# Weights of differential attention by head: each head's attention between the projections of the next

## The chip, the cores and the metric

One NeuronCore of a Trainium2 chip runs the whole program in one launch. The metric is the device time of that launch in microseconds (us), and of the kernel before three runs are given. PE is the matrix engine (TensorE), DVE the vector engine, ACT the scalar engine, POOL the general one; SP is the queue that issues the DMA loads.

## The reference, cut to what matters

The program is a model of four layers: differential attention with a SwiGLU layer, an RWKV-7 mixer with a mixture of experts, and two layers of sparse attention beside a gated recurrence. The change touches only the first, an attention over `T` = 272 positions (16 meta tokens and 256 inputs) of width 1024 with 8 heads:

```python
qkv = jnp.einsum('bld,de->ble', x, w_in)
q, k, v = jnp.split(qkv, 3, axis=-1)
q = q.reshape(B, Lp, H, 2, Dh)          # 8 heads, 2 halves of 64
k = k.reshape(B, Lp, H, 2, Dh)
vf = v.reshape(B, Lp, H, Dv)            # 8 heads of 128
s = jnp.einsum('bqhcd,bkhcd->bhcqk', qblk, k) * scale
s = s - slopes[None, :, None, None, None] * dist
p = jax.nn.softmax(s, axis=-1)
a = p[:, :, 0] - lam * p[:, :, 1]
o = jnp.einsum('bhqk,bkhe->bqhe', a, vf)
o = o * lax.rsqrt(jnp.mean(o * o, -1, keepdims=True) + SUBLN_EPS) * subln_g * (1.0 - lam_init)
return jnp.einsum('ble,ed->bld', o.reshape(B, L, H * Dv), w_o)
```

## The kernel before, in words

Every engine has one list of instructions, written out by a function per layer (`attention_pe`, `attention_act`, `attention_dve`), and runs it in order. An engine waits only for counters (semaphores) that others raise. `bank` gives a product one of the eight PSUM banks, `b=` a fixed one, and a new owner waits until the one before has been read.

A projection is computed from operands that are split in two parts each: `high` lets ACT round a 128x1024 piece of weights to fp32r (`wh`, L301), `low` lets DVE take the rest (`wl`, L310), and `mm3` adds up three fp32r matmuls (L158 to L160). A unit of 128 output columns is 8 chunks of the contraction times 3, thus 24 matmuls of 272 columns. `H`, the input, lies transposed in 8 chunks and is split in the same way into `at_xs`. Weights come as a stream, `SA`: SP loads 1 MB into one of 3 raw slots, which are two pieces, and a raw slot is free again when `low` has run on its last piece. The split pieces have 4 places (`NPART`), and a place is free when the unit that used it is done.

The first layer runs in three stages, one behind the other:

1. The start. SP issues the parameters (`PAR`), constants (`CB`), all of `H`, three loads of weights and `dist` (the distances). ACT and DVE split `H`, then four pieces; PE waits for both.
2. The projections. 16 units make q and k (transposed, `at_q`, `at_k`), the first four of them chunk by chunk together (`project_units`). Then v is made the other way round, positions on the partitions (`at_v`): four groups of 256 columns, 3 blocks of positions (`QT`: 96, 96, 80), 72 matmuls of 256 columns each.
3. The attention loop over 24 items (8 heads times 3 blocks of query positions). Per item PE makes two scores (`scores`, L558), DVE adds the distances and takes the row maximum (`first`, L705 to L711), ACT takes exponentials (`exps`, L634), DVE combines the two softmaxes (`second`, L721 to L727), PE transposes the result (`turned`, L569) and ACT copies it (L646, L647). Once per head PE multiplies with v (`values`, L577), DVE copies the result (`keep`, L731) and ACT squares it (L655). PE runs `scores` three items ahead of `turned`.

Then 8 matmuls add up the squares of all heads (L594), DVE and ACT make the factors (L741 to L745), PE spreads them (L600), DVE scales the heads (L748), and the output projection begins (`attn_o`). `busy_pe` (L420) is a helper that issues plain fp32 matmuls of 512 columns whose result nobody reads; the norm behind the layer uses it.

## Time and profile before

| What | us |
|---|---|
| median of 3 runs (2877.8 to 2885.52) | 2882.27 |
| the profiled execution | 2887.5 |
| its span, from the first to the last instruction | 2885.7 |
| of it: until PE's first matmul | 19.2 |
| projections of q, k and v, until the first scores | 85.4 |
| attention loop and sums of squares, until the factors | 100.8 |

The last three rows are the stretches at 0 to 19.2, 19.2 to 104.6 and 104.6 to 205.4 us. The other 2680 us of the span, from the factors on, are the rest of this layer and the three others. Sums and durations from the trace belong to the profiled execution, which is 5.2 us above the median.

### The profile page before, as it was taken

To read this page: it belongs to the slowest core of one execution; us is meant where nothing else is said; L and a number is where in the kernel's file an instruction comes from. 1 tells how busy PE (TensorE), PEld (TensorE's weight loads), DVE (VectorE), ACT (ScalarE), POOL (GpSimd) and SP (SyncE) were. 2 spreads that over 40 slices of the span, in tenths; PEclk is the share of its full clock that TensorE was granted. 3 is DMA by queue.
4 is the path that set the end of the run, shared out by engine and by line. 5 is a ranking of instruction groups with operands and counts; after the bars stand their busy time and mean duration, and the time that the engine had idled before them with its cause. 6 is when DMAs were issued, how large, how long until landed. Compare 5 with 4: busy or idle time off the path is not lost.

```text
span 2885.7 us, 49498 instructions
## 1 busy us (share of the span) xinstructions
PE 2687.2 (93%) x21078; PEld 2216.2 (77%) x21078; DVE 2045.1 (71%) x2943; ACT 1541.5 (53%) x2245; POOL 101.4 (4%) x124
## 2 busy tenths in 40 slices
PE   7779999999898999999999999998999989999988
PEld 7649997688876766666666666667969988978977
DVE  4565546664435889898898989895856865757864
ACT  3334442622123777777777777774446454446443
POOL 0000000010003100000000000000000101000001
PEclk9759999999988999999999999999999999999999
DMA  6203553300022799898999989893525634524532
GB/s 206 74 0 117 176 171 98 108 21 4 4 102 75 297 348 349 332 364 335 344 352 348 351 330 364 333 346 102 153 58 149 186 113 123 154 80 145 167 118 96
DMA packets 244413, 547.66 MB, mean 190 GB/s; under 512 B 24492, under 2 KB 187784, under 8 KB 200924
## 3 DMA queue, kind: packets, MB, share of 16 engines
q1 hardware_dynamic: 242204, 541.54, 53.3%
q8 instruction: 169, 2.77, 0.4%
q0 software_dynamic: 1984, 2.89, 0.4%
q14 instruction: 56, 0.46, 0.0%
HBM read 540.46 MB, written 1.05 MB: 188 GB/s over the span
## 4 chain that ended last, share of the span: by engine, by line
PE 75%; DVE 15%; ACT 6%; issue 2%; DMA 2%; DVEq 0%; SPq 0%; ACTq 0%
PE PS L158 20%; PE PS L160 20%; PE PS L159 20%; DVE wl L310 3%; ACT wh L301 3%; PE PS L1066 1%; PE PS L349 1%; PE PS L2379 1%; PE PS L1810 1%; PE PS L577 1%; DVE mix L1359 1%; DMA raw<-in_w_in 1%; DVE mix L1357 1%; PE PS L1836 1%; PE PS L1094 1%
## 5 line engine op out<-in xcount | busy, mean ns | idle before, releaser
L310 DVE TENSOR_TENSOR wl<-raw,wh 128x1024 fp32r<-128x1024 f32 (+2 forms) x630 | 746.3, 1189 | 411.5 <-ACT wh L301 392.7
L301 ACT ACTIVATE wh<-raw 128x1024 fp32r<-128x1024 f32 (+2 forms) x630 | 643.9, 1026 | 582.6 <-PE PS L160 534.5
L310 DVE TENSOR_TENSOR wl<-early,wh 128x1024 fp32r<-128x1024 f32 x384 | 466.8, 1225 | 55.6 <-ACT wh L301 35.2
L301 ACT ACTIVATE wh<-early 128x1024 fp32r<-128x1024 f32 x384 | 407.0, 1061 | 127.7 <-PE PS L160 118.7
L158 PE MATMUL PS<-b_hn_h,wh 128*128 128x256 f32 (+2 forms) x1312 | 378.5, 288 | 15.1 <-DVE wl L310 8.9
L160 PE MATMUL PS<-b_hn_h,wl 128*128 128x256 f32 (+2 forms) x1312 | 372.3, 284 | 0.0
L159 PE MATMUL PS<-b_hn_l,wh 128*128 128x256 f32 (+2 forms) x1312 | 371.7, 283 | 0.0
L158 PE MATMUL PS<-wh,xe_h 128*96 128x512 f32 x896 | 357.3, 399 | 1.2 <-DVE xe_l L1962 1.2
L160 PE MATMUL PS<-wh,xe_l 128*96 128x512 f32 x896 | 353.7, 395 | 0.0
L159 PE MATMUL PS<-wl,xe_h 128*96 128x512 f32 x896 | 353.4, 394 | 0.0
L158 PEld LDWEIGHTS PS<-b_hn_h,wh 128*128 128x128 f32 (+2 forms) x1312 | 233.4, 178 | 20.6 <-DVE wl L310 10.5
L159 PEld LDWEIGHTS PS<-b_hn_l,wh 128*128 128x128 f32 (+2 forms) x1312 | 233.2, 178 | 0.7
L160 PEld LDWEIGHTS PS<-b_hn_h,wl 128*128 128x128 f32 (+2 forms) x1312 | 233.1, 178 | 0.3
L160 PEld LDWEIGHTS PS<-wh,xe_l 128*96 128x96 f32 x896 | 144.8, 162 | 63.6
L158 PEld LDWEIGHTS PS<-wh,xe_h 128*96 128x96 f32 x896 | 145.1, 162 | 61.1 <-DVE xe_l L1962 1.5
L159 PEld LDWEIGHTS PS<-wl,xe_h 128*96 128x96 f32 x896 | 145.4, 162 | 59.3
L158 PE MATMUL PS<-wh,mh_h 128*96 128x512 f32 x448 | 177.8, 397 | 0.0
L160 PE MATMUL PS<-wh,mh_l 128*96 128x512 f32 x448 | 177.0, 395 | 0.0
L159 PE MATMUL PS<-wl,mh_h 128*96 128x512 f32 x448 | 175.8, 392 | 0.0
L158 PE MATMUL PS<-ff_x_h,wh 128*128 128x272 f32 x352 | 102.1, 290 | 0.5 <-DVE ff_x_l L486 0.3
L160 PE MATMUL PS<-ff_x_h,wl 128*128 128x272 f32 x352 | 101.8, 289 | 0.0
L349 PE MATMUL PS<-mix,raw 128*128 128x272 f32 x384 | 95.4, 410 | 6.8 <-DVE mix L1359 4.0
(473 smaller groups left out, 5127.8 us busy)
## 6 DMA issues: line engine op xcount, KB each, us to landing
early<-in_moe_in SPq DMA_DIRECT2D x128, 1024.0 KB, 4.8
raw<-in_moe_in SPq DMA_DIRECT2D x96, 1024.0 KB, 4.8
early<-in_moe_out SPq DMA_DIRECT2D x64, 1024.0 KB, 4.8
raw<-in_w_in SPq DMA_DIRECT2D x56, 1024.0 KB
raw<-in_moe_out SPq DMA_DIRECT2D x48, 1024.0 KB, 4.9
raw<-in_w_in SPq DMA_DIRECT2D x32, 704.0 KB
raw<-in_attn_w_in SPq DMA_DIRECT2D x12, 1024.0 KB, 5.5
raw<-in_rw_w_rkv SPq DMA_DIRECT2D x12, 1024.0 KB, 5.0
```

Source lines behind the costliest of these rows:

```text
L158: e.matmul(o, wh, xh, start=start, stop=False)
L159: e.matmul(o, wh, xl, start=False, stop=False)
L160: return e.matmul(o, wl, xh, start=False, stop=stop)
L301: act.e.activation(st.two(n)[0], st.raw(n), ACT.Copy).then_inc(*act.sig("hi", st.name, n, sem=f"hi_{st.name}"))
L310: dve.e.tensor_tensor(lo, st.raw(n), hi.bitcast(F32), SUB).then_inc(*dve.sig("lo", st.name, n, sem=f"lo_{st.name}"))
L349: t = pe.e.matmul(PS[:, b, 0:Tn], cols_view(256)(st.slot(m))[:, k, c:c + 128], X[:, k, :], start=k == 0, stop=k == KC - 1)
L577: t = e.matmul(PS[:, b, 0:T], at_v[0:kn, kt, h * 128:(h + 1) * 128], at_t[h % 2][0:kn, kt, :], start=kt == 0, stop=kt == 2)
L1066: x = e.matmul(PS[p:p + CB_, b, f * CB_:(f + 1) * CB_], lhsT[p:p + CB_, f, :], rhs[p:p + CB_, f, :], start=True, stop=True)
L1094: x = e.matmul(PS[p:p + CB_, b, f * CB_:(f + 1) * CB_], a_[d][p:p + 64, f, t], b_[d][p:p + 64, f, t], start=True, stop=True)
L1357: e.scalar_tensor_tensor(X, rw_e[:, k, 1:T + 1], par("mu", 48 + i * 8 + k), H[:, k, :], MUL, SUB).then_inc(*dve.own())
L1359: e.scalar_tensor_tensor(X, rw_e[:, k, 0:T], par("mu", i * 8 + k), X, MUL, SUB).then_inc(*dve.sig("mixed", i, k))
L1810: t = e.matmul(PS[0:CAP, b, :], P1[:, i, e_, :], Ht[x][:, i, c], start=i + x == 0, stop=i + x == 3)
```

## The change

Weights of q, k and v come in a stream of their own, `SQ`, in 24 loads of 128 columns (512 KB, one piece each) into six half slots, in the order q, k, v of head 0, then of head 1, and so on. v of a head is now projected as q and k are, into `at_u` (head by position); PE transposes it in three blocks (`v_turned`) and ACT copies them to `at_v` (`v_taken`). The old v matmuls are gone: 288 of 256 columns are replaced by 192 of 272 columns and 24 transposes.

`attention_order` is PE's list: 32 steps; step `i` holds the unit `i` of the 24 and the item `n = i - 3`: `scores(n)`, `unit(i)`, for every third step `v_turned`, `values` or `sums`, and `turned(n - 2)`. ACT and DVE have loops of the same steps, with the evacuation of all units on ACT. The banks are fixed: scores 0 and 1, transposes 2, values 3, units 4 and 5, the sums of squares 6, turned v 7. The sums of squares are taken head by head. Behind them stand four matmuls of `busy_pe`.

At the start `H` comes in four parts, with the first two pieces of weights between them; `PAR` and `CB` come behind the third piece. Only two units are made chunk by chunk, and PE waits for the constants only before the first transpose.

```diff
+            a = self.after
+            return a and ("lo", a.name, len(a.pieces) - len(a.slots) + 2 * m + 1)
...
-    SA = Stream("A", RAW, PARTS)
-    projection(SA, "qk", A["attn_w_in"][0], 0, 2 * D)
-    for u in range(4):
-        by_half(SA, ("v", u), A["attn_w_in"][0], 2 * D + u * 256, 256)
+    SQ = Stream("Q", [x[:, c:c + 1024] for x in RAW for c in (0, 1024)], PARTS)
+    UNITS = [(what, h) for h in range(8) for what in ("aq", "ak", "av")]
+    for what, h in UNITS:
+        by_cols(SQ, (what, h), A["attn_w_in"][0], ("aq", "ak", "av").index(what) * D + h * 128, 128)
+    SA = Stream("A", RAW, PARTS, after=SQ)
     projection(SA, "attn_o", A["attn_w_o"][0], 0, D)
...
         if n >= len(st.parts):
             act.wait_ge(act.at("used", st.name, n - len(st.parts)))
+        elif st.after:
+            act.wait_ge(act.at("used", st.after.name, len(st.after.pieces) - len(st.parts) + n))
         act.e.activation(st.two(n)[0], st.raw(n), ACT.Copy).then_inc(*act.sig("hi", st.name, n, sem=f"hi_{st.name}"))
...
+    at_u = [tile(f"at_u{n}", T) for n in range(2)]
     ITEMS = [(h, i) for h in range(8) for i in range(3)]
+
+    def attention_order(unit, v_turned, scores, turned, values, sums):
+
+
+        for i in range(len(UNITS) + 8):
+            n = i - 3
+            if 0 <= n < len(ITEMS):
+                scores(n)
+            if i < len(UNITS):
+                unit(i)
+            if i >= 3 and i % 3 == 0 and i <= len(UNITS):
+                v_turned(i // 3 - 1)
+            if n >= 5 and n % 3 == 2 and n // 3 <= 8:
+                values(n // 3 - 1)
+            if 2 <= n < len(ITEMS) + 2:
+                turned(n - 2)
+            if n >= 7 and n % 3 == 1 and n // 3 <= 9:
+                sums(n // 3 - 2)
 
     def attention_pe(pe):
         e = pe.e
-        pe.wait_ge(pe.at("consts"))
         pe.wait_ge(pe.at("psum_zero"))
-        for _ in project_units(pe, SA, "qk", [("qk", u) for u in range(4)], at_xs, T, ("x_lo", "attn")):
-            pass
-        for u in range(4, 16):
-            project_unit(pe, SA, "qk", u, 128, at_xs, T)
-        for u in range(4):
-            bs = [bank("v", u, i) for i in range(3)]
-            for k0 in (0, 4):
-                n, (wh, wl) = piece(pe, SA)
-                for i, (q0, qn) in enumerate(QT):
-                    if k0 == 0 and bs[i][1]:
-                        pe.wait_ge(pe.at(*bs[i][1]))
-                    for k in range(4):
-                        t = mm3(e, PS[0:qn, bs[i][0], 0:256], at_xs[0][:, k0 + k, q0:q0 + qn],
-                                at_xs[1][:, k0 + k, q0:q0 + qn], wh[:, k, :], wl[:, k, :], k0 + k == 0, k0 + k == KC - 1)
-                    if k0 and i < 2:
-                        t.then_inc(*pe.sig("v_mm", u, i))
-                t.then_inc(*used(pe, SA, n))
-            pe.also("v_mm", u, 2)
+
+        def unit(i):
+            what, h = UNITS[i]
+            if i == 0:
+                for _ in project_units(pe, SQ, "", UNITS[0:2], at_xs, T, ("x_lo", "attn"), (4, 5)):
+                    pass
+            elif i > 1:
+                project_unit(pe, SQ, what, h, 128, at_xs, T, b=4 + i % 2)
+
+        def v_turned(h):
+            b, before = bank("v_rows", h, b=7)
+            if before:
+                pe.wait_ge(pe.at(*before))
+            pe.wait_ge(pe.at("consts"))
+            pe.wait_ge(pe.at("av", h))
+            for kt, (k0, kn) in enumerate(QT):
+                t = e.transpose(PS[0:kn, b, kt * 128:(kt + 1) * 128], at_u[h % 2][:, k0:k0 + kn], ident)
+            t.then_inc(*pe.sig("v_rows_mm", h))
 
...
+            pe.wait_ge(pe.at("aq", h))
+            pe.wait_ge(pe.at("ak", h))
             for c in range(2):
-                b, before = bank("scores", n, c, b=(n % 2) * 2 + c)
-                pe.wait_ge(pe.at(*before))
+                b, before = bank("scores", n, c, b=c)
+                if before:
+                    pe.wait_ge(pe.at(*before))
...
-            b, before = bank("turned", n, b=4 + n % 2)
-            pe.wait_ge(pe.at(*before))
+            b, before = bank("turned", n, b=2)
+            if before:
+                pe.wait_ge(pe.at(*before))
             pe.wait_ge(pe.at("diff", n))
...
-            b, before = bank("attn_v", h, b=6 + h % 2)
-            pe.wait_ge(pe.at(*before))
+            b, before = bank("attn_v", h, b=3)
+            if before:
+                pe.wait_ge(pe.at(*before))
             pe.wait_ge(pe.at("turned", 3 * h + 2))
+            pe.wait_ge(pe.at("v_rows", h))
...
-        pe.wait_ge(pe.at("qk", 14))
-        pe.wait_ge(pe.at("qk", 15))
-        for n in range(len(ITEMS) + 6):
-            if n < len(ITEMS):
-                scores(n)
-            if n >= 6 and n % 3 == 0:
-                values(n // 3 - 2)
-            if 3 <= n < len(ITEMS) + 3:
-                turned(n - 3)
-        b, before = bank("subln")
-        pe.wait_ge(pe.at(*before))
-        for h in range(8):
+        def sums(h):
+            if h == 0:
+                bank("subln", b=6)
             pe.wait_ge(pe.at("at_sq", h))
-            t = e.matmul(PS[0:8, b, 0:T], one_of_8[:, 7 - h:15 - h], at_sq[:, h, :], start=h == 0, stop=h == 7)
-        t.then_inc(*pe.sig("subln_mm"))
+            t = e.matmul(PS[0:8, 6, 0:T], one_of_8[:, 7 - h:15 - h], at_sq[:, h, :], start=h == 0, stop=h == 7)
+            if h == 7:
+                t.then_inc(*pe.sig("subln_mm"))
+
+        attention_order(unit, v_turned, scores, turned, values, sums)
+        busy_pe(pe, 4, "subln", at=7)
...
-        act.wait_ge(act.at("h_in"))
-        split_act(act, "attn", H, at_xs[0])
-        for n in range(NPART):
-            high(act, SA)
+
+        def x_high(k):
+            act.wait_ge(act.at("h_in", k // 2))
+            e.activation(at_xs[0][:, k, :], H[:, k, :], ACT.Copy).then_inc(*act.sig("x_hi", "attn", k))
+
+        for k in range(2):
+            x_high(k)
+        for n in range(2):
+            high(act, SQ)
+        for k in range(2, KC):
+            x_high(k)
+        high(act, SQ)
...
-        for u in range(16):
-            high(act, SA)
-            if u % 2:
-                act.wait_ge(act.at("qk.mm", u))
-                e.activation((at_q if u < 8 else at_k)[:, u % 8, :], ps("qk", u), ACT.Copy).then_inc(*act.sig("qk", u))
-        for u in range(4):
-            high(act, SA)
-            high(act, SA)
-            for i, (q0, qn) in enumerate(QT):
-                act.wait_ge(act.at("v_mm", u, i))
-                e.activation(at_v[0:qn, i, u * 256:(u + 1) * 256], ps("v", u, i, p=qn, n=256), ACT.Copy).then_inc(
-                    *act.sig("v", u, i))
+
+        def evacuated(i):
+            what, h = UNITS[i]
+            act.wait_ge(act.at(what + ".mm", h))
+            if what == "av" and h >= 2:
+                act.wait_ge(act.at("v_rows_mm", h - 2))
+            dst = at_u[h % 2] if what == "av" else (at_q if what == "aq" else at_k)[:, h, :]
+            e.activation(dst, ps(what, h), ACT.Copy).then_inc(*act.sig(what, h))
+
+        def v_taken(h):
+            act.wait_ge(act.at("v_rows_mm", h))
+            src = PS[0:96, bank_of["v_rows", h], 0:384].rearrange("p (a b) -> p a b", a=3)
+            e.activation(at_v[0:96, :, h * 128:(h + 1) * 128], src, ACT.Copy).then_inc(*act.sig("v_rows", h))
...
-        for n in range(len(ITEMS) + 6):
-            if n < len(ITEMS):
-                exps(n)
-            if n >= 7 and n % 3 == 1:
-                h = n // 3 - 2
-                act.wait_ge(act.at("attn_v", h))
-                e.activation(at_sq[:, h, :], at_o[:, h, :], ACT.Square).then_inc(*act.sig("at_sq", h))
+        def sums(h):
+            act.wait_ge(act.at("attn_v", h))
+            e.activation(at_sq[:, h, :], at_o[:, h, :], ACT.Square).then_inc(*act.sig("at_sq", h))
+
+        for i in range(len(UNITS) + 8):
+            n = i - 3
+            if 1 <= i <= len(UNITS):
+                evacuated(i - 1)
+            if i >= 4 and i % 3 == 1 and i <= len(UNITS) + 1:
+                v_taken(i // 3 - 1)
             if 3 <= n < len(ITEMS) + 3:
                 turned(n - 3)
+            if i + 3 < len(UNITS):
+                high(act, SQ)
+            elif i < len(UNITS) + 1:
+                high(act, SA)
+            if 0 <= n < len(ITEMS):
+                exps(n)
+            if n >= 6 and n % 3 == 0 and n // 3 <= 9:
+                sums(n // 3 - 2)
...
+
+        def x_low(k):
+            dve.wait_ge(dve.at("x_hi", "attn", k))
+            e.tensor_tensor(at_xs[1][:, k, :], H[:, k, :], at_xs[0][:, k, :].bitcast(F32), SUB).then_inc(
+                *dve.sig("x_lo", "attn", k))
+
+        for k in range(2):
+            x_low(k)
+        for n in range(2):
+            low(dve, SQ)
+        for k in range(2, KC):
+            x_low(k)
+        low(dve, SQ)
         dve.wait_ge(dve.at("consts"))
-        dve.wait_ge(dve.at("h_in"))
-        split_dve(dve, "attn", H, *at_xs)
-        for n in range(NPART):
-            low(dve, SA)
...
-        for u in range(16):
-            low(dve, SA)
-            if u % 2 == 0:
-                dve.wait_ge(dve.at("qk.mm", u))
-                e.tensor_copy((at_q if u < 8 else at_k)[:, u % 8, :], ps("qk", u)).then_inc(*dve.sig("qk", u))
-        for u in range(4):
-            low(dve, SA)
-            low(dve, SA)
-        dve.wait_ge(dve.at("dist"))
...
+            dve.wait_ge(dve.at("dist"))
             dve.wait_ge(dve.at("scores_mm", n))
...
+        for i in range(len(UNITS) + 8):
+            n = i - 3
+            if 0 <= n < len(ITEMS):
                 first(n)
             if 1 <= n <= len(ITEMS):
                 second(n - 1)
-            if n >= 7 and n % 3 == 1:
+            if i + 3 < len(UNITS):
+                low(dve, SQ)
+            elif i < len(UNITS) + 1:
+                low(dve, SA)
+            if n >= 6 and n % 3 == 0 and n // 3 <= 9:
                 keep(n // 3 - 2)
...
     def sync(sp):
         e = sp.e
+        for c in range(4):
+            e.dma_start(flat(H[:, 2 * c:2 * c + 2, :]), A["hT"][:, 2 * c * T:(2 * c + 2) * T]).then_inc(
+                *sp.sig("h_in", c, by=16, sem=f"h_in{c}"))
+            if c < 2:
+                load(sp, SQ)
+        load(sp, SQ)
         e.dma_start(PAR, A["par"]).then_inc(*sp.sig("consts", by=16))
         e.dma_start(CB, A["c_base"]).then_inc(*sp.sig("consts", by=16))
-        e.dma_start(flat(H), A["hT"]).then_inc(*sp.sig("h_in", by=16))
+        load(sp, SQ)
+        e.dma_start(flat(dist), A["c_dist"]).then_inc(*sp.sig("dist", by=16))
+        while sp.piece["Q"] < len(SQ.loads):
+            load(sp, SQ)
         for m in range(NRAW):
             load(sp, SA)
-        e.dma_start(flat(dist), A["c_dist"]).then_inc(*sp.sig("dist", by=16))
```

How the order moves, in three places. First SP's queue from its start (`raw_53` to `raw_55` are the three raw slots), before:

```order
L2882 DMA PAR<-in_par 128x777
L2883 DMA CB<-in_c_base 128x592
L2884 DMA H<-in_hT 128x2176
L290 DMA raw_53<-in_attn_w_in 128x8x256
L290 DMA raw_54<-in_attn_w_in 128x8x256
L290 DMA raw_55<-in_attn_w_in 128x8x256
L2887 DMA dist<-in_c_dist 128x816
L290 DMA raw_53<-in_attn_w_in 128x8x256
```

and with the change:

```order
L2933 DMA H<-in_hT 128x544
L293 DMA raw_53<-in_attn_w_in 128x8x128
L2933 DMA H<-in_hT 128x544
L293 DMA raw_53<-in_attn_w_in 128x8x128
L2933 DMA H<-in_hT 128x544 x2
L293 DMA raw_54<-in_attn_w_in 128x8x128
L2938 DMA PAR<-in_par 128x777
L2939 DMA CB<-in_c_base 128x592
L293 DMA raw_54<-in_attn_w_in 128x8x128
L2941 DMA dist<-in_c_dist 128x816
L293 DMA raw_55<-in_attn_w_in 128x8x128 x2
```

`H` and the first two pieces now stand ahead of the constants, and a load has half the columns.

Second DVE in the middle of the attention, from one item's scores to the next (`at_s_72` and so on are buffers of the items, `wl_57` to `wl_63` the four places of split weights), before:

```order
L705 SCALAR_TENSOR_TENSOR at_s_72<-dist,PS 96x544 [waits attn_mm_pe]
L709 TENSOR_REDUCE at_x_86<-at_s_72 96x2 [waits attn_dve]
L711 TENSOR_SCALAR at_x_86<-at_x_86 96x2 [waits order_dve]
L721 RECIPROCAL at_x_89<-at_x_89 96x2 [waits attn_dve,attn_act]
L723 TENSOR_SCALAR at_x_89<-at_x_89,lam 96x1 [waits order_dve]
L725 TENSOR_SCALAR at_c_83<-at_e_79,at_x_89 96x272 [waits order_dve]
L727 SCALAR_TENSOR_TENSOR at_c_83<-at_e_79,at_x_89,at_c_83 96x272 [waits order_dve]
L705 SCALAR_TENSOR_TENSOR at_s_73<-dist,PS 80x544 [waits attn_mm_pe]
```

and with the change:

```order
L750 SCALAR_TENSOR_TENSOR at_s_73<-dist,PS 80x544 [waits attn_mm_pe]
L754 TENSOR_REDUCE at_x_87<-at_s_73 80x2 [waits attn_dve]
L756 TENSOR_SCALAR at_x_87<-at_x_87 80x2 [waits order_dve]
L766 RECIPROCAL at_x_86<-at_x_86 96x2 [waits attn_dve,attn_act]
L768 TENSOR_SCALAR at_x_86<-at_x_86,lam 96x1 [waits order_dve]
L770 TENSOR_SCALAR at_c_80<-at_e_76,at_x_86 96x272 [waits order_dve]
L772 SCALAR_TENSOR_TENSOR at_c_80<-at_e_76,at_x_86,at_c_80 96x272 [waits order_dve]
L315 TENSOR_TENSOR wl_63<-raw_55,wh_62 128x1024 [waits hi_Q]
L750 SCALAR_TENSOR_TENSOR at_s_74<-dist,PS 96x544 [waits attn_mm_pe]
```

Each item now has one `low` of weights behind it.

Third PE at the end of a head. Before, from `values`:

```order
L577 MATMUL PS<-at_t_84,at_v 128x272 [waits attn_act]
L577 MATMUL PS<-at_t_84,at_v 128x272 x2
L569 MATMUL PS<-CB,at_c_83 96x96 [waits attn_dve]
L569 MATMUL PS<-CB,at_c_83 96x96
L569 MATMUL PS<-CB,at_c_83 80x96
L558 MATMUL PS<-at_k,at_q 96x272 [waits attn_dve]
L558 MATMUL PS<-at_k,at_q 96x272
L569 MATMUL PS<-CB,at_c_80 96x96 [waits attn_dve]
L569 MATMUL PS<-CB,at_c_80 96x96
```

with the change, from the last matmul of a unit:

```order
L162 MATMUL PS<-at_x_h,wl_57 128x272
L606 MATMUL PS<-at_t_84,at_v 128x272 [waits attn_act]
L606 MATMUL PS<-at_t_84,at_v 128x272 x2
L596 MATMUL PS<-CB,at_c_83 96x96 [waits attn_dve]
L596 MATMUL PS<-CB,at_c_83 96x96
L596 MATMUL PS<-CB,at_c_83 80x96
L584 MATMUL PS<-at_k,at_q 96x272 [waits attn_dve]
L584 MATMUL PS<-at_k,at_q 96x272
L160 MATMUL PS<-at_x_h,wh_58 128x272 [waits lo_Q]
```

Before, `values` stands behind scores alone; now a whole unit stands ahead of it, and another behind the next scores.

## Rows read from the trace of the kernel before

**Rows 1.** Page, part 4: shares of the chain that ended last, by engine

```profile
PE 75%; DVE 15%; ACT 6%; issue 2%; DMA 2%; DVEq 0%; SPq 0%; ACTq 0%
```

**Rows 2.** Busy time by stretch: length, each engine (records), PE clock, DMA share, GB/s

```profile
0.00:19.20 19.20, 0.00 (x0) 0.01 (x1) 11.30 (x14) 7.95 (x13) 0.20 (x4) 1.00 0.93 306
19.20:104.60 85.40, 85.16 (x673) 84.79 (x673) 31.70 (x37) 28.96 (x41) 0.00 (x0) 1.00 0.48 155
104.60:205.40 100.80, 69.79 (x233) 35.59 (x232) 70.44 (x178) 42.33 (x157) 0.00 (x0) 0.54 0.04 11
2292.00:2322.00 30.00, 26.93 (x212) 25.24 (x211) 19.48 (x49) 17.63 (x42) 11.18 (x22) 1.00 0.57 175
```

**Rows 3.** Timeline, 8 to 20 us: start, length, instruction [idle before <- releaser]

```profile
9.49 2.66 ACT L501 ACTIVATE at_x_h<-H 128x272 fp32r<-128x272 f32 x8 [7.48 <-DMA H<-in_hT]
...
15.51 2.00 ACT L301 ACTIVATE wh<-raw 128x1024 fp32r<-128x1024 f32 x2 [1.01 <-DMA raw<-in_attn_w_in]
...
16.60 2.36 DVE L310 TENSOR_TENSOR wl<-raw,wh 128x1024 fp32r<-128x1024 f32 x2 [0.65 <-ACT wh L301]
...
19.22 0.56 PE L158 MATMUL PS<-at_x_h,wh 128*128 128x272 f32 x1 [19.22 <-DVE wl L310]
```

**Rows 4.** DMA issues: count, KB each, median us from issue to landing

```profile
raw<-in_rw_a SPq DMA_DIRECT2D x2, 256.0 KB, 3.6
...
PAR<-in_par SPq DMA_DIRECT2D x1, 388.5 KB, 3.2
```

**Rows 5.** Timeline, PE at 20 to 25.5 us and ACT in the projections

```profile
20.03 0.43 PE L158 MATMUL PS<-at_x_h,wh 128*128 128x272 f32 x1
20.26 0.43 PE L159 MATMUL PS<-at_x_l,wh 128*128 128x272 f32 x1
...
25.45 0.29 PE L158 MATMUL PS<-at_x_h,wh 128*128 128x272 f32 x1
...
40.78 1.06 ACT L301 ACTIVATE wh<-raw 128x1024 fp32r<-128x1024 f32 x1 [1.89 <-PE PS L160]
...
46.80 1.06 ACT L301 ACTIVATE wh<-raw 128x1024 fp32r<-128x1024 f32 x1 [1.89 <-PE PS L160]
```

**Rows 6.** Timeline, PE in the attention loop, around one head's end

```profile
139.94 0.71 PE L569 MATMUL PS<-CB,at_c 96*96 96x96 f32 x3
140.58 1.20 PE L558 MATMUL PS<-at_k,at_q 64*80 64x272 f32 x4
...
146.60 3.09 PE L577 MATMUL PS<-at_t,at_v 96*128 96x272 f32 x6 [3.10 <-ACT at_t L647]
```

**Rows 7.** Timeline, DVE in the attention loop, one item

```profile
143.08 0.43 DVE L731 COPY at_o<-PS 128x272 f32<-128x272 f32 x1
143.43 0.71 DVE L705 SCALAR_TENSOR_TENSOR at_s<-dist,PS 80x544 f32<-80x544 f32 x1
...
146.44 0.71 DVE L705 SCALAR_TENSOR_TENSOR at_s<-dist,PS 96x544 f32<-96x544 f32 x1
```

**Rows 8.** Timeline, DVE and PE from the last item's scores to the output projection

```profile
188.69 0.70 DVE L705 SCALAR_TENSOR_TENSOR at_s<-dist,PS 80x544 f32<-80x544 f32 x1
...
192.71 0.50 DVE L727 SCALAR_TENSOR_TENSOR at_c<-at_e,at_x,at_c 80x272 f32<-80x272 f32 x1
...
205.36 0.43 DVE L741 TENSOR_SCALAR n<-PS 8x272 f32<-8x272 f32 x1 [4.67 <-PE PS L594]
...
194.74 1.88 PE L569 MATMUL PS<-CB,at_c 96*96 96x96 f32 x9
...
200.14 5.18 PE L594 MATMUL PS<-at_sq,CB 128*8 128x272 f32 x16
208.51 6.45 PE L600 MATMUL PS<-r,CB 8*128 8x272 f32 x16 [3.18 <-DVE r L745]
214.88 0.59 PE L158 MATMUL PS<-at_x_h,wh 128*128 128x272 f32 x1
```

**Rows 9.** Timeline, PE, 512-column fp32 matmuls of busy_pe behind the norm

```profile
250.89 1.45 PE L426 MATMUL PS<-CB 128*128 128x512 f32 x3
```

More of the change, by code:

```diff
@@ L55 @@
     "ln": "ln_centred ln_var ln_sq ln_root ln_scaled",
-    "attn": "lam_dots lam_exp subln subln_r subln_o subln_root at_sq attn_v scores row_max diff exps turned",
-    "attn_mm": "v_mm scores_mm turned_mm attn_v_mm subln_mm subln_o_mm",
+    "attn": "lam_dots lam_exp subln subln_r subln_o subln_root at_sq attn_v scores row_max diff exps turned aq ak av v_rows",
+    "attn_mm": "v_rows_mm scores_mm turned_mm attn_v_mm subln_mm subln_o_mm",
     "k_norm": "k_k k_sq k_norm k_norm_root k_norm_r k_spread",
@@ L115, with __init__ @@
 class Stream:
-    def __init__(self, name, slots, parts):
-        self.name, self.slots, self.parts = name, slots, parts
+    def __init__(self, name, slots, parts, after=None):
+        self.name, self.slots, self.parts, self.after = name, slots, parts, after
         self.loads, self.pieces, self.of = [], [], {}
@@ L143, in freed @@
         if before < 0:
-            return None
+            a = self.after
+            return a and ("lo", a.name, len(a.pieces) - len(a.slots) + 2 * m + 1)
         pieces = self.loads[before][1]
@@ L731, in keep @@
             e.tensor_copy(at_o[:, h, :], ps("attn_v", h)).then_inc(*dve.sig("attn_v", h))
-        for n in range(len(ITEMS) + 6):
-            if n < len(ITEMS):
+        for i in range(len(UNITS) + 8):
+            n = i - 3
+            if 0 <= n < len(ITEMS):
                 first(n)
@@ L2881, in sync @@
         e = sp.e
+        for c in range(4):
[4 more added lines that the diff above has]
+        load(sp, SQ)
         e.dma_start(PAR, A["par"]).then_inc(*sp.sig("consts", by=16))
         e.dma_start(CB, A["c_base"]).then_inc(*sp.sig("consts", by=16))
-        e.dma_start(flat(H), A["hT"]).then_inc(*sp.sig("h_in", by=16))
+        load(sp, SQ)
+        e.dma_start(flat(dist), A["c_dist"]).then_inc(*sp.sig("dist", by=16))
+        while sp.piece["Q"] < len(SQ.loads):
+            load(sp, SQ)
         for m in range(NRAW):
             load(sp, SA)
-        e.dma_start(flat(dist), A["c_dist"]).then_inc(*sp.sig("dist", by=16))
         if stages < 3:
-            for m in range(NRAW, 20 if stages == 1 else 20 + 30):
+            for m in range(NRAW, 8 if stages == 1 else 8 + 30):
                 load(sp, SA)
```

## The prediction

> **What bounds the kernel now.** I read the page's chain first. PE holds 75% of what ended last [rows 1], so an edit pays where it takes PE time or PE waits away. Then I cut the first layer into its stretches [rows 2]. Up to 19.2 us PE does nothing. In the next 85.4 us it is busy for 85.2, and DVE and ACT for about a third. In the following 100.8 us, the attention loop, PE is busy for only 69.8, and its granted clock is 0.54 where it was 1.00 before: most of that stretch runs at the lower level, 1.2 GHz, so even the 69.8 are about twice what the same work takes at 2.4 GHz. DVE is busy for 70.4 and ACT for 42.3. What PE waits for is seen once per head: 3.10 us ahead of `values`, for ACT's copy of the last transposes [rows 6], because a chain of PE, DVE, ACT, DVE, PE, ACT has to be walked and PE has nothing else to do. So one stretch has PE full and DVE idle, the next has the chain as its bound and a slow PE. The change lays one over the other.
>
> **The start.** Before, `H` is there for ACT at 9.49, the second pair of weight pieces is begun at 15.51 and PE begins at 19.22, behind four `low` [rows 3]. The change needs only two pieces and `H` in front. How fast is the queue? The whole first stretch moves 306 GB/s on the mean [rows 2]; without some 2.5 us in which nothing moves yet that is about 0.35 MB per us. `PAR`, 0.40 MB, lands 3.2 us after its issue at 0.7 [rows 4]; 1.1 of that is its bytes, so 2.1 is fixed. By this, `H` parts 1 and 2 with two pieces (1.6 MB) land at 0.7 + 2.1 + 4.6 = 7.4. The same reckoning puts the end of the 1.8 MB up to `H` before at 8.0, where ACT had it at 9.49, so I add 1.5: 8.9. Then `high` 1.0 and `low` 1.2, halves of a pair [rows 3]: PE begins at 11.1, 8.1 earlier. The unknown is the packet of 512 bytes (128 columns) in place of 1 KB. Nearest row: `rw_a`, 256 KB in packets of 256 bytes, 1024 of them as in a piece here, lands in 3.6 us [rows 4], where fixed part and bytes give 2.8. So a piece costs between nothing and 0.8 more, and at the very worst as much as 1 MB, 1.4 more. I take nothing, as 512 bytes lie nearer to 1 KB in bytes per packet; the other end puts the start at 13.9.
>
> The Trainium skill, "DMA: Bandwidth & Descriptors", section Specifications, gives 512 bytes as the smallest transfer that runs at line rate. By that rule the start stays at 11.1 us; by the bound from the rows it would be up to 2.8 later.
>
> Once started, PE's matmuls come 0.23 apart until about 25.4, 6.2 us after the first, some 27 of them, and from then on a unit of 24 takes (46.80 - 40.78) / 2 = 3.01, 0.125 each [rows 5]. The same ramp is paid after. Units 0 to 2 are 72 matmuls: 6.2 + 45 x 0.125 = 11.8, so the first scores begin at 22.9.
>
> **The 21 steps with unit and item.** PE's share of each piece at full clock is half of its row in the loop [rows 6]: scores 1.20 / 2 = 0.6, transposes 0.64 / 2 = 0.32 (the next instruction starts 0.64 after them), `values` 3.09 / 2 = 1.55. The transposes of v are new: three blocks of 128 columns where 96 take 0.32, so 0.43; the other end is that they don't gain from the clock, 0.85. A sum of squares is 5.18 / 8 = 0.65 [rows 8], I take 0.45. The steps hold 21 units (63.2), 21 scores (12.6), 19 transposes (6.1), 7 turned v (3.0), 6 `values` (9.3) and 5 sums (2.3): 96.5 us, 4.6 per step.
>
> Does DVE keep up? An item costs it 3.01 from start to start [rows 7], a `low` 1.18 [rows 3], `keep` 0.43 [rows 7], once per three steps: 21 x 4.19 + 5 x 0.43 = 90.2, 4.3 per step. It fits, by 6%. ACT is busy 42.3 in the old loop and gets 1.0 for `high`, 0.4 for an evacuation and a sixth of a microsecond for v per step: about 3.3. Do the chains fit? `turned(n - 2)` stands at the end of step n, some 2.8 steps or 12.9 us after its scores began; scores 0.7, first 1.65, exponentials 1.1 and the place of `second` behind the next `first` need about 8.2. `values` comes after a whole unit, 3.0 us, which covers the 3.10 wait. The wait for `lo` is covered by three steps, that for a load by about six (0.5 MB per 4.6 us is 114 GB/s, a third of the rate). A unit's bank is read one step before it is wanted. If any of these covers went, its wait would stand open on PE. So the steps end at 22.9 + 96.5 = 119.4.
>
> **The tail.** Three items are left without units: the first of them starts on DVE at 120.1, and two items with one `low` and one `keep` put item 23 at 127.7. Before, from there to the factors was 205.36 - 188.69 = 16.7 us [rows 8]. Two parts of it go: the transposes of three items queue behind `values` and end at 196.6, 3.4 us after the last `second` at 193.2; alone they need 0.64 (2.7 less). And DVE waits 4.67 for eight sums; the square and one sum are 1.1 (3.5 less). That gives 127.7 + 10.5 = 138.2, at the lower clock, as before. **Gain so far: 205.4 - 138.2 = 67.2 us.**
>
> **Behind the sums.** Before, PE idles 3.18 for the factors, spreads them in 6.45 and starts the output projection at 214.88, at the lower clock [rows 8]. Now four matmuls of 512 columns fill the wait. Two records are one matmul; they follow 0.43 apart at the full clock [rows 9]: 3.4 in all, hidden. At half clock they are 6.9 and delay the factors by 3.7. In return they can give the spreading at full clock (up to 2.8 less) and the first 21 matmuls of the projection (2.1 less, 0.1 each). Between +3.7 and -4.6 I take 0. The three other layers have the same instructions; the banks rotate from another start, so that a few waits there ask for another bank. I cost that at nothing, up to 2 us either way: such waits ask for work one unit or more back.
>
> **Sum:** 2887.5 - 67.2 = 2820.3 for the profiled execution, which stood 5.2 above the median: **2815 us**.
>
> **Rivals.** (A) *DVE becomes the bound.* It is in order: each step it may have to wait for PE's scores, as it does once per head now, and then `low` stands behind it. If 0.7 us of each step are such a wait, a step is 5.0 and 21 steps 105 (+9); with the 1.8 that the copy of a head's scores waits now, in every third step or more, up to 5.4 (+18). For it: only 6% of room. Against: PE's scores stand first in their step and wait for nothing late. 2824 to 2833; chance 0.15.
>
> (B) *PE stays at the lower clock among small pieces: slower than before.* The loop of now is at 0.54 with its short matmuls. At half clock a unit is 24 x 0.23 = 5.5 and the rest doubles: 21 x 5.5 + 66.6 = 182, 86 more: 2901, 19 slower. It decides from 7.8 us per step (4.6 + 67 / 21); half clock would be 8.7. Against it: in the last layers the same pattern, a head's attention between projections, stands at 2292 to 2322 with PE busy for 26.9 of 30 us and a clock of 1.00 [rows 2]. Chance 0.04. The Trainium skill, "TensorE: Matmul & The Clock Gate", section "A second HAM failure mode: psum-queue depth-cycling", tells of a kernel whose PE idles briefly between groups as PSUM banks come round, so that its clock swings between both levels; that would be this rival. Row 2292 speaks against it.
>
> (C) *The overlap doesn't come about*, as one wait holds every step back until the chain has been walked: the gain is then only the start and the cheaper v (85.4 us less 16 units of 3.01 and 2.8 for the ramp leaves 34 for v; 8 units are 24, and the transposes 3), 8 + 7: 2867. All waits that I followed have a step or more of room. Chance 0.04.
>
> **Chances and range.** The forecast with its bounds (start +2.8; transposes of v +3; behind the sums +3.7 or -4.6; tail at full clock, `values` and scores, -3; other layers 2 either way) has 0.77 and goes from 2805 to 2826. To leave out no more than 2 in 10, the range reaches over (A): 2804 to 2834. A difference of 0.3%, 9 us, is about what can be told from no change. Faster 0.95, within it 0.01, slower 0.04.
>
> **What would show it.** PE's first matmul near 11 us; first scores near 23; scores of successive items 4.6 apart with 4.2 and 5.4 in turn; granted clock 1.00 to about 119; PE busy over 95% there and DVE about 90%; the factors' first instruction near 138; the output projection near 148. (A) shows as PE waiting for `diff` or `lo`, DVE without idle time; (B) as 0.23 between a unit's matmuls. I am wrong if steps take over 5.2 us, or if the gain is lost again behind 140 us.

## The result and the profile after

The changed kernel takes **2841.4 us** (median of four runs, 2837.0 to 2842.7), the kernel before 2880.0 on the same chip (four runs, 2876.2 to 2885.5). The ratio is 0.9861, 95% interval 0.9844 to 0.9878: 38.6 us faster. I had forecast 2815 in a range of 2804 to 2834. The sign is right, the size is not, and the time lies outside the range.

The profiled execution of the change took 2837.0 us, with a span of 2835.2 and a mean granted clock of 0.969. It is the fastest of its kernel's runs, and the one shown of before (2887.5) is slower than all four above, so the two executions are 50.5 us apart where the medians are 38.6 apart. The traces tell where the difference lies, the medians how large it is.

The first layer in stretches: windows of the change, to be held against [rows 2]. Columns as there.

```profile
0.00:10.80 10.80, 0.00 (x0) 0.01 (x1) 6.84 (x6) 5.64 (x10) 0.20 (x4) 1.00 0.89 268
10.80:21.70 10.90, 10.88 (x74) 10.73 (x74) 7.60 (x16) 5.32 (x9) 0.00 (x0) 1.00 1.13 317
21.70:119.80 98.10, 98.10 (x713) 83.05 (x712) 83.22 (x170) 61.91 (x175) 0.00 (x0) 1.00 0.45 130
119.80:141.60 21.80, 13.44 (x50) 6.42 (x48) 11.89 (x29) 9.21 (x30) 0.00 (x0) 0.67 0.16 48
```

The stretch from the first scores to the last step is 98.1 us. PE is busy in all of it at a granted clock of 1.00, where the old loop had 0.54. DVE is busy for 83.2 of it.

The start: timeline of the change, beside [rows 3].

```profile
5.37 1.06 ACT L306 ACTIVATE wh<-raw 128x1024 fp32r<-128x1024 f32 x1 [0.99 <-DMA raw<-in_attn_w_in]
8.25 1.06 ACT L306 ACTIVATE wh<-raw 128x1024 fp32r<-128x1024 f32 x1 [1.82 <-DMA raw<-in_attn_w_in]
9.33 1.23 DVE L315 TENSOR_TENSOR wl<-raw,wh 128x1024 fp32r<-128x1024 f32 x1 [1.65 <-ACT wh L306]
10.82 0.57 PE L160 MATMUL PS<-at_x_h,wh 128*128 128x272 f32 x1 [10.82 <-DVE wl L315]
```

The second piece, in packets of 512 bytes, is there for ACT at 8.25, where the forecast had 8.9. The smaller packets cost nothing that can be seen here.

Three steps of PE in the middle of the stretch, timeline; the units stand in the gaps between the rows shown.

```profile
42.16 0.69 PE L584 MATMUL PS<-at_k,at_q 64*80 64x272 f32 x4
45.88 1.54 PE L606 MATMUL PS<-at_t,at_v 96*128 96x272 f32 x6
47.26 0.41 PE L596 MATMUL PS<-CB,at_c 96*96 96x96 f32 x3
47.60 0.70 PE L584 MATMUL PS<-at_k,at_q 64*96 64x272 f32 x4
51.34 0.49 PE L572 MATMUL PS<-CB,at_u 128*96 128x128 f32 x3
51.66 0.41 PE L596 MATMUL PS<-CB,at_c 96*96 96x96 f32 x3
52.00 0.70 PE L584 MATMUL PS<-at_k,at_q 64*96 64x272 f32 x4
55.74 0.37 PE L596 MATMUL PS<-CB,at_c 80*96 80x80 f32 x3
56.04 0.62 PE L614 MATMUL PS<-at_sq,CB 128*8 128x272 f32 x2
56.60 0.69 PE L584 MATMUL PS<-at_k,at_q 64*80 64x272 f32 x4
```

From scores to scores (L584) it is 5.44, 4.40 and 4.60 us: a step with `values`, one with the transposes of v (L572), one with a sum of squares (L614). `values` takes 1.54, half of the 3.09 of [rows 6]. No row has a wait.

The tail and the sums: PE's timeline of the change, beside [rows 8].

```profile
134.98 0.64 PE L596 MATMUL PS<-CB,at_c 80*96 80x80 f32 x3 [2.08 <-ACT at_t L680]
135.55 1.08 PE L614 MATMUL PS<-at_sq,CB 128*8 128x272 f32 x2
136.55 3.09 PE L606 MATMUL PS<-at_t,at_v 96*128 96x272 f32 x6
140.64 1.07 PE L614 MATMUL PS<-at_sq,CB 128*8 128x272 f32 x2 [1.00 <-ACT at_sq L684]
141.64 4.92 PE L431 MATMUL PS<-CB 128*128 128x512 f32 x8
146.49 3.93 PE L624 MATMUL PS<-r,CB 8*128 8x272 f32 x16
150.35 0.39 PE L160 MATMUL PS<-at_x_h,wh 128*128 128x272 f32 x1
```

The output projection begins at 150.35, 64.5 us ahead of its 214.88 in [rows 8]. That is the forecast of 67 within 3 us. **What is missing from the forecast was lost behind it.** The table follows single instructions of DVE through both traces, and through the first experiment, which is told below. The first three columns are their starts, the last two how much earlier than before.

| instruction, place | before | change | e1 | change earlier | e1 earlier |
|---|---|---|---|---|---|
| `rw`, end of the preparation of the scan | 591.90 | 526.09 | 528.17 | 65.8 | 63.7 |
| `mh_l`, head of the experts' layer | 989.46 | 930.73 | 918.83 | 58.7 | 70.6 |
| `Yl`, its end | 1959.78 | 1900.81 | 1888.96 | 59.0 | 70.8 |
| `wl`, in the last two layers | 2448.72 | 2393.90 | 2376.21 | 54.8 | 72.5 |
| `b_rms_s`, the end | 2875.42 | 2824.87 | 2799.37 | 50.6 | 76.1 |

Two places give time back in the change: between the first row and the second, the recurrent layer with its scan, 7.1 us, and behind the third, the last two layers, 8.4. Through the experts' layer, 970 us, nothing moves. In e1 the same two places gain.

### The profile page after: what moved, and what is told of

Its sections match the earlier page's. It is cut to its first block, busy times and chain, and to the rows that moved or that the text cites. A ratio compares the mean times of both kernels' runs of the same rounds, so it can differ in the third digit from the quotient of the medians.

```text
span 2835.2 us, 49373 instructions
## 1 busy us (share of the span) xinstructions
PE 2660.0 (94%) x21014; PEld 2201.3 (78%) x21014; DVE 2039.8 (72%) x2935; ACT 1543.4 (54%) x2257; POOL 97.0 (3%) x124
## 4 chain that ended last, share of the span: by engine, by line
PE 77%; DVE 13%; ACT 6%; issue 2%; DMA 1%; DVEq 0%; SPq 0%; ACTq 0%
PE PS L160 20%; PE PS L162 19%; PE PS L161 19%; DVE wl L315 4%; ACT wh L306 3%; PE PS L354 2%; PE PS L1116 2%; DMA raw<-in_w_in 1%; PE PS L1144 1%; PE PS L1860 1%; PE PS L2429 1%; PE PS L1886 1%; PE PS L1153 1%; PE PS L2401 1%; DVE b_cx L2811 1%
## 5 line engine op out<-in xcount | busy, mean ns | idle before, releaser
L160 PEld LDWEIGHTS PS<-b_hn_h,wh 128*128 128x128 f32 (+2 forms) x1312 | 233.5, 178 | 21.9 <-DVE wl L315 11.1
L161 PE MATMUL PS<-ff_x_l,wh 128*128 128x272 f32 x352 | 101.3, 288 | 0.0
```

Of the source, the lines that this page charges most:

```text
L160: e.matmul(o, wh, xh, start=start, stop=False)
L161: e.matmul(o, wh, xl, start=False, stop=False)
```

## What changed behind the first layer: a counter

The code there is the same, but what `bank` deals out is not. It deals the eight banks from a running counter, `turn[0] % 8`. Before, the counter stood at 29 ahead of the factors; in the change, with fixed banks for units, turned v and sums, it stands at 0. So every product after that which takes its bank from the counter lies three banks further round, while the ones with a fixed bank (`b=`) stay. Where both kinds meet, a product now gets a bank with another owner, and PE, in order, waits until that owner has been read.

One such place in full: in each of the last two layers PE makes `ma` in banks 4 to 7 (L2456), then `rnn` in the same banks, which DVE reads last of all (`rnn_gate`, L2871), then the units `out_a` (L2502) from the counter. PE's timeline of the change there:

```profile
2318.12 0.28 PE L162 MATMUL PS<-b_hc,wl 128*128 128x256 f32 x1
2321.23 0.36 PE L160 MATMUL PS<-b_o,wh 128*128 128x256 f32 x1 [2.83 <-DVE b_m L2871]
```

PE's 2.83 us of idle time are for the first bank of `out_a`, which is one of those four. Windows of the change around it, 4 us each:

```profile
2316.00:2320.00 4.00, 2.40 (x21) 2.19 (x19) 2.00 (x3) 2.88 (x4) 0.00 (x0) 1.00 0.77 241
2320.00:2324.00 4.00, 2.77 (x15) 2.80 (x16) 2.08 (x5) 2.70 (x2) 0.00 (x0) 0.73 0.59 184
2324.00:2328.00 4.00, 4.00 (x31) 4.00 (x30) 0.93 (x1) 1.06 (x1) 0.00 (x0) 0.84 0.29 99
```

The granted clock was 1.00, falls to 0.73 on the mean of the stretch in which PE comes back, and is 0.84 in the next one: 31 matmuls in 4 us against 37 at full clock. So the wait of 2.8 us costs more than 2.8: 0.27 and 0.16 of 4 us each are another 1.7, by estimate. The windows of e1 at the same place:

```profile
2303.80:2307.80 4.00, 4.00 (x37) 4.00 (x36) 2.01 (x3) 2.87 (x4) 0.00 (x0) 1.00 0.76 248
2307.80:2311.80 4.00, 4.00 (x37) 4.00 (x36) 2.31 (x6) 3.64 (x3) 0.00 (x0) 1.00 0.59 189
```

The Trainium skill, "TensorE: Matmul & The Clock Gate", section "A second HAM failure mode: psum-queue depth-cycling", describes a kernel that goes round the PSUM banks, in which PE idles briefly so often that its clock swings between both levels. I had held it against the interleaved steps, where the clock stayed at 1.00. Here, where I had not looked, the 0.73 behind one wait for a bank agrees with it in kind; this is a single wait of 2.83 us and not a frequent short one.

## Experiments

Two theories stood at the start. **Banks:** the 27 us missing are the counter's. **Others:** they come from where the drops of PE's clock fall, whatever the banks, or they are a consequence of the change in the first layer itself (the idle matmuls, the order of the loads, transfers that arrive at other times). All edits are on the changed kernel unless it says otherwise. Ratios are against the kernel before, run on the same chip, with 95% intervals.

**e1: the counter set back to what it was.** From the output projection on, every wait then asks for the same bank and owner as before.

```diff
         busy_pe(pe, 4, "subln", at=7)
+        turn[0] = 29
         pe.wait_ge(pe.at("subln_r"))
```

> The changed kernel, with the rotation of the PSUM banks set, behind the sums of squares, to where it stood in the kernel before (29 banks taken), so that every later wait for a bank asks for the same owner as before. Theory 1 (the 65 us gained in the first layer are partly lost behind it because the banks rotate from another start and PE waits for other banks in the RWKV scan and the last layers): the instructions behind the first layer run 64 to 66 us earlier than before to the very end, and the total gain is 60 to 67 us (about 2817). Theory 2 (the later loss comes from where the drops of the matrix engine's clock fall, whatever the banks): the gain stays near 40 us (2835 to 2845), with the same loss behind 530 us. Theory 3 (the later layers are tied to loads that do not move with the first layer): also near 40 us.

Measured 2814.0 us (five runs, 2811.5 to 2823.7), ratio 0.9784 (0.9764 to 0.9804). One line that computes nothing is worth 27.4 us by the medians; the two ratios, 0.9861 and 0.9784, are 22 us apart, the two traces 25.5. It is also the time that I had forecast for the change.

**e2: the counter alone, in the kernel before.**

```diff
+        turn[0] = 32
         pe.wait_ge(pe.at("subln_r"))
```

> The kernel before, with only the rotation of the PSUM banks set behind the sums of squares to where the changed kernel has it (a multiple of 8). Theory 1 (banks): slower than before by 20 to 27 us, 2900 to 2907, with the loss in the RWKV scan and the last layers. Theory 2 (clock drops) and theory 3 (loads): no difference beyond 5 us from before.

Measured 2898.8 us (six runs, 2897.1 to 2907.5), ratio 1.0074 (1.0056 to 1.0092). 32 deals bank 0 next, as the change does; there is nothing else of the change in it, and it is about 20 us slower by the medians. In the traces, where before stands with one of its longer executions, e2 loses 3.4 us in the recurrent layer and 9.8 behind 2100 us, the two places that were expected. PE's waits between 2320 and 2400 us, first e2, then before:

```profile
PE PS L158 <- DVE b_m L2822: 4.1, 2, 2.8
```

```profile
PE PS L158 <- DVE b_m L2821: 1.7, 1, 1.7
```

The second wait of e2 stands ahead of `out_a`, as long as in the change; before has none there, its 1.7 stands ahead of a matmul of `rnn`:

```profile
2381.14 0.36 PE L158 MATMUL PS<-b_o,wh 128*128 128x256 f32 x1 [2.83 <-DVE b_m L2822]
```

So the rotation makes it, not the new first layer. e1 and e2 together decide for the banks.

**e3: without the idle matmuls** (the `busy_pe` line removed).

> The changed kernel without its four idle matmuls behind the sums of squares. In its trace they ran from 141.6 to 146.5 us and the factors were spread in 3.9 us at the full clock; before, spreading took 6.5. All theories: without them spreading starts 1.5 to 2 us earlier but takes 6.5 us, and the first 20 matmuls of the output projection are at the lower clock: the output projection starts 1 us later to 1 later, and its first units end 1 to 3 us later. Total within 3 us of the changed kernel, if the later layers do not react.

Measured 2836.2 us (2835.6 to 2838.2), ratio 0.9849 (0.9829 to 0.9868): not to be told from the change. Its trace has what was to be seen, PE idle for the factors and their spreading at half speed:

```profile
145.53 7.62 PE L623 MATMUL PS<-r,CB 8*128 8x272 f32 x16 [3.18 <-DVE r L794]
```

It ends at 153.2 where the change has its first projection at 150.35, and 400 us into the trace it is 3.8 us later than the change. Of that only 0.9 is left at the head of the experts' layer, and the median is 5 us better than the change's. One pair of executions can't price so small a part: e5 below, the same code as the change up to the last two layers, is 10.0 us ahead of it at 720 us and 3.7 at the head of the experts' layer. e10 puts the question again where the scan has the banks of before.

**e4: the loads in the old order** (at the start `PAR`, `CB`, the four parts of `H`, then four pieces of `SQ`).

> The changed kernel with SP's queue at the start in the old order: parameters and constants, then H in its four parts, then four pieces of weights, then the distances. From 0.35 MB per us the two first pieces land after 2.85 MB, 3.5 us later than in the change. All theories: PE's first matmul at 14 to 15 us in place of 10.8, everything behind it equally later, total 3 to 4 us slower than the changed kernel.

Measured 2840.5 us (2837.2 to 2840.9), ratio 0.9861 (0.9841 to 0.9881). In the trace PE begins at 14.06, as expected, and the layers behind the first are 3.7 us later than in the change at 400 us and 3.9 at the end, with less than 1 us in the middle of the scan; yet the median is the same. Medians taken at different times differ by some 3 us for reasons of their own (before's own are 2878.9 to 2882.3); a part of that size is read from the trace's start only.

**e5: the counter of before from the last two layers on.**

```diff
     def second_pe(pe, l):
+        if l == 0:
+            turn[0] = 647
         e = pe.e
```

> The changed kernel, with the rotation of the banks set as in the kernel before only from the first of the two last layers on; the RWKV scan keeps the changed rotation. Theory 1a (the loss has two places that add up: 12 us in the scan, 14 in the last two layers, as the traces of the change and of e1 stand against each other): 2826 us, give or take 3. Theory 1b (the loss in the last layers only follows from the state in which the scan leaves the kernel): no better than the change, 2838 to 2843.

Measured 2825.3 us (2820.0 to 2830.0), ratio 0.9813 (0.9797 to 0.9829): by the medians 16.1 us of the 27.4 are in the last two layers. In the trace e5 gains 13.3 us on the change behind the head of the experts' layer.

**e6: `out_a` in banks that are free**, each unit in bank `u`, the counter left as the change has it.

```diff
-            projected(pe, l, "out_a", u, oT)
+            projected(pe, l, "out_a", u, oT, b=u)
```

> The changed kernel with one stage of the last layers on fixed banks: the eight units of out_a take banks 0 to 7 in order, so that the first four of them do not ask for the banks of the contraction rnn, which DVE reads last. The rotation elsewhere is that of the change (eight banks more or less are a full turn). In the trace of the change PE waits 2.83 us for that read, its clock falls, and out_a ends about 5 us later than in e1, in each of the two layers. Theory 1 (this one wait is most of the loss in the last layers): 9 to 11 us faster than the change, 2830 to 2833. Rival (the loss is spread over many small waits): within 3 us of the change.

Measured 2827.4 us (2824.8 to 2830.2), ratio 0.9813 (0.9798 to 0.9828). One call with a fixed bank is worth 14.0 us by the medians; I had expected 9 to 11. Each of the two ratios carries 4 to 5 us of uncertainty, and the two traces are only 8.0 apart, 3.8 of it at the first `out_a` and 4.3 at the second. So this one set of waits is at least half of what the last two layers lose, and by the medians nearly all. PE's waits for `b_m` in both last layers (2200 us to the end), first in the change, then in e6:

```profile
PE PS L160 <- DVE b_m L2871: 9.4, 4, 3.5
```

```profile
PE PS L160 <- DVE b_m L2871: 2.7, 2, 1.5
```

The two that are gone are those ahead of `out_a`, 2.83 and 3.49 us. Part of this comes back a little later, at the first unit of `out`, in both layers; here the first of them, in the change, then in e6:

```profile
2348.26 0.36 PE L160 MATMUL PS<-b_q_r,wh 128*128 128x256 f32 x1 [2.66 <-DVE wl L315]
```

```profile
2344.41 0.36 PE L160 MATMUL PS<-b_q_r,wh 128*128 128x256 f32 x1 [3.43 <-DVE b_cx L2895]
```

With 0.8 us more there in each layer, 4.8 us of the 8.0 are waiting. The other 3.2 fit the clock: in e6 it is 1.00 between 2316 and 2332 us, where the change loses 1.7 by the estimate above, and at the second `out_a` (2768 to 2776 us) the change has 0.62 and 0.95, again 1.7. Where the rest of the 14.0 is, no trace shows.

**e9: the other half, the counter of before for the scan and the experts alone** (`turn[0] = 29` as in e1, and the change's own value, 618, at the head of `second_pe`).

> The complement of e5: the changed kernel with the banks as in the kernel before from the sums of squares to the end of the mixture of experts, so in the scan, and the changed rotation again in the two last layers. If the two places add up (theory 1a), e5's gain of 16 us over the change and this one's make up e1's 27: 2828 to 2832. If the scan's loss is not its own (theory 1b): 2838 to 2843.

Measured 2827.6 us (2825.3 to 2832.3), ratio 0.9822 (0.9803 to 0.9841): 13.8 us. With e5's 16.1 that is 29.9 against e1's 27.4, so the two places are separate and together are the whole. The traces agree more closely: e9 is 12.1 us ahead of the change at the head of the experts' layer and 11.8 at the end, which with e5's 13.3 makes 25 against e1's 25.5. As the experts' layer moved by nothing in the table, this part belongs to the recurrent layer. Not all of it is the scan: e9 is 7.7 us ahead of the change at 720 us, 5.7 at 800 and 12.1 at 860, and e1 likewise (7.4, 5.7, 12.0), so that a part comes behind the scan, where I followed no wait. PE's longest waits in the scan, 590 to 740 us in the change:

```profile
PE PS L1098 <- ACT rw_ru L1353: 10.7, 1, 10.7
...
PE PS L1144 <- DVE sc_lb L1508: 2.7, 1, 2.7
PE PS L1177 <- DVE sc_lb L1508: 2.7, 1, 2.7
```

and in e1, 570 to 725 us:

```profile
PE PS L1099 <- ACT sc_pad L1327: 9.6, 1, 9.6
...
PE PS L1145 <- DVE sc_lb L1509: 0.9, 1, 0.9
PE PS L1191 <- DVE sc_lb L1509: 0.9, 1, 0.9
```

Two waits for DVE's `sc_lb` are 2.7 where they were 0.9. They ask for the fixed banks 4 to 7, which the transposes of the scan (`forward`) take and DVE reads. One stands ahead of the same line in both kernels (L1144, in e1 L1145); the other ahead of `upd` (L1177) in the change and ahead of `y` (L1191), which PE issues later, in e1. They give 3.6 us and the first row 1.1. What follows the first of them in the change is the clock:

```profile
598.76 1.53 PE L1177 MATMUL PS<-rw_ru,sc_n 56*56 56x64 f32 x24 [2.71 <-DVE sc_lb L1508]
```

```profile
594.00:598.00 4.00, 1.89 (x14) 1.70 (x14) 1.84 (x3) 0.10 (x1) 0.00 (x0) 1.00 0.00 0
598.00:602.00 4.00, 3.24 (x61) 3.25 (x63) 3.45 (x16) 0.60 (x1) 0.00 (x0) 0.51 0.02 4
602.00:606.00 4.00, 4.00 (x94) 4.00 (x92) 0.00 (x0) 0.60 (x1) 0.00 (x0) 0.63 0.00 0
```

Windows of 40 us, the change first, then about the same work in before:

```profile
594.80:634.80 40.00, 34.87 (x1002) 34.31 (x1003) 17.19 (x42) 12.48 (x24) 0.00 (x0) 0.88 0.01 3
```

```profile
660.00:700.00 40.00, 36.22 (x1175) 35.45 (x1171) 17.16 (x42) 14.84 (x28) 0.00 (x0) 1.00 0.02 4
```

PE is busy for about as long and gets 1002 matmuls done instead of 1175. The traces of e3, e4, e5 and e6, which have the change's counter in the scan, show the same wait of 2.7 us and behind it a 4 us window at 0.57 to 0.66; those of before, e1, e7 and e9 have the 0.9, and the clock stays at 1.00 there. Behind the second wait the clock falls in the change, e3 and e4 but not in e5 and e6: the same wait does not cost the same in every execution. No run gave the scan's products fixed banks one by one, so what each wait is worth in time stays open.

**e7: e1 and e6 together.**

> e1 (the banks as before from the sums of squares on) with out_a on banks 0 to 7. In e1 only the first unit of out_a was free of the wait; now four are. Theory 1: between e1 and 3 us better, 2811 to 2815. A version that could be kept.

Measured 2816.0 us (2808.2 to 2818.7), ratio 0.9762 (0.9747 to 0.9777). It can't be told from e1: with the counter of before, the first `out_a` units already find free banks, and e1's waits for `b_m` (3.1 us) are hardly more than e6's.

**e8: e7 with another start, 27.**

> As e7, but the rotation two banks further back (27 in place of 29), which no kernel here has had. out_a no longer depends on it. Theory 1 says only that the scan reacts to the rotation: between e7 and 12 us slower, 2812 to 2826. If it is as fast as e7, the scan's loss belongs to the one rotation of the change; if faster, the rotation of the kernel before was not the best.

Measured 2819.8 us (2819.0 to 2823.1), ratio 0.9791 (0.9776 to 0.9806), 4 us behind e7 by the medians, 8 by the ratios, whose intervals just touch. With `out_a` fixed, this start costs little, but it doesn't beat the old one.

**e10: e7 without the idle matmuls.**

> e7 without the four idle matmuls behind the sums of squares, to price this term where nothing behind it reacts. e3's trace had the rest of the program 3.8 us later than the change's, but its median was 5 us better than the change's in another call. If the matmuls pay (they keep the clock up for the spreading and the output projection): 1 to 4 us slower than e7, 2817 to 2820. If not: 2811 to 2815.

Measured 2823.1 us (2820.4 to 2826.7), ratio 0.9799 (0.9781 to 0.9817), against e7's 0.9762: in this pair they are worth 7 us by the medians and 11 by the ratios, where I had expected 1 to 4. In the traces e10 is 3.2 us later at 400 us, of which the spreading explains 2.3 (it ends at 152.6 instead of 150.3). The lag is about 0 at 560 us, 3.2 again at 1963, and 6.9 at 2800. So what is shown of them is 3 to 4 us where they stand (e3 and e10). What they are worth in the whole stays open: 7 us here, nothing in the change against e3.

## Why the prediction was wrong, and where it was right

The order follows the prediction.

- **Start.** PE at 10.8 (forecast 11.1), first scores at 21.7 (22.9). Right, and the end of the range with slow small packets is excluded.
- **Steps.** (119.82 - 21.68) / 21 = 4.67 us (forecast 4.6), the last at 119.8 (119.4). PE never idle, clock 1.00. The pieces at half of their row in the old loop came out at 0.69 for scores (0.60) and 1.54 for `values` (1.55).
- **DVE** was forecast at 90.2 of the 96.5 us and took 83.2 of 98.1. Rival A (DVE as the bound) asked for PE waiting on `diff` or `lo`; PE waited for nothing there, and DVE idled 8.6 us for PE's scores:

```profile
DVE at_s L750 <- PE PS L584: 8.6, 11, 1.3
```

- **Rival B** (a slow PE among small pieces) asked for a step of 7.8 and a low clock: 4.67 and 1.00. **Rival C** (no overlap) asked for 2867 us, 52 more than the forecast, with PE held by a wait in every step. Both are out.
- **Tail.** The factors begin 3.5 us later than forecast, at 141.75, not 138.2: item 23 was on DVE at 129.23, not 127.7, and from there it took 12.5, not 10.5, as DVE's timeline shows:

```profile
129.23 0.72 DVE L750 SCALAR_TENSOR_TENSOR at_s<-dist,PS 80x544 f32<-80x544 f32 x1 [1.05 <-PE PS L584]
...
133.26 0.50 DVE L772 SCALAR_TENSOR_TENSOR at_c<-at_e,at_x,at_c 80x272 f32<-80x272 f32 x1
...
141.75 0.43 DVE L791 TENSOR_SCALAR n<-PS 8x272 f32<-8x272 f32 x1 [1.63 <-PE PS L614]
```

  The term of 10.5 was too small by 2, in two places that the rows of the tail above show. The transposes do take only 0.64, but they begin 1.2 us behind the last `second` (133.26 and 0.50 long), because all transposes now share bank 2 and ACT had first to copy the ones before ([2.08 <-ACT at_t L680]). Behind them a sum of squares (1.08) stands ahead of the last `values`.
- **Behind the sums.** I took 0 between +3.7 and -4.6. The idle matmuls took 4.9 us, mostly beside DVE's work, and the spreading 3.93 in place of 6.45 [rows 8]. The output projection then stood 64.5 us ahead, against a sum of 67.2.
- **"The three other layers have the same instructions; the banks rotate from another start, so that a few waits there ask for another bank. I cost that at nothing, up to 2 us either way."** This is the step that failed. It was 27.4 us by the medians (e1; 22 by the ratios), and about 20 alone (e2). I named the mechanism and gave as its price that "such waits ask for work one unit or more back". That holds between products of the counter, eight of them apart. It does not hold where they meet products in fixed banks, whose reader may be among the latest instructions of DVE, as `rnn_gate` is: 2.83 and 3.49 us of wait ahead of `out_a`, and a lower clock behind. The order of the instructions with their waits was there to be compared over the whole program, and the row that would have priced it was in the trace: how late DVE reads `rnn`.

With the counter set back, e1 was 64.9 us faster than before (2878.9 to 2814.0; 56 to 68 by the ratio's interval), against the 67.2 of the sum. That its 2814.0 meets the 2815 to a microsecond is luck, as before's own median was 3 us lower there; that the rest of the sum holds within its uncertainty is not. In the traces e1 goes on gaining behind the first layer (63.7 to 76.1). At least a part of that is the execution shown of before, 5.2 us above its median.

## What to carry to other kernels

A counter that deals buffers out is state of the whole program: an edit that takes a different number from it re-deals every buffer behind it. Compare the waits of the whole program, not only of the edited part, and price each that has changed its owner by how late that owner is read. Where such products meet ones in fixed banks, give them fixed banks too, or set the counter back behind the edit: here that made 0.9861 into 0.9784 (e1), or 0.9762 with `out_a` fixed as well (e7). e7 is the one I would keep, as its `out_a` no longer depends on the counter; that it is faster than e1 is not shown (2816.0 against 2814.0 by the medians, and the intervals overlap).

A stretch in which a chain of engines leaves PE idle, beside one in which PE is full, can be laid over it: here PE's clock went from 0.54 to 1.00 by that, and the sums of squares were read at 141.8 us in place of 205.4. Single banks that serve while units stand between their products can hold the chain where the units are gone, as bank 2 did in the tail.

## What the runs showed of the hardware that I had not expected

- A single idle time of 2.83 us on PE between two stretches of dense matmuls is followed by 4 us at a mean granted clock of 0.73 and 4 at 0.84. In the scan, a wait of 2.7 us is followed by a window at 0.51 to 0.66 in five traces, and one of 0.9 at the same work leaves it at 1.00 in four.
- Two executions of the same code can be 9 us apart over one scan of some 200 us (the change against e5), and the same wait is followed by a fall of the clock in one and not in the other.
- Four matmuls that compute nothing (eight records), beside a wait of 3.18 us for the factors, let the spreading run in 3.93 us in place of 7.62, and the work behind it begins 3 to 4 us earlier. In the whole they were worth 7 us in one pair (e7 against e10) and nothing in another (the change against e3).
- Loads of 512 KB in packets of 512 bytes, 24 of them, landed in 5.3 us (median), those of 1 MB in packets of 1 KB before in 5.5. Both were queued behind others, so these are no times of a load alone; the first layer's start showed no loss.
